# Causal attention on one Trainium2 core: scores, probabilities and their transposes cut to the visible keys

## What is computed

```python
def _causal_softmax(logits, q_pos, k_pos):
    mask = k_pos[None, :] <= q_pos[:, None]
    logits = jnp.where(mask, logits.astype(jnp.float32), -1e30)
    return jax.nn.softmax(logits, axis=-1)

# block 1, latent attention: 8 heads, 96 wide, values 64 wide, 272 keys
s = jnp.einsum('bqhd,bkhd->bhqk', qb, k) * scale
out = jnp.einsum('bhqk,bkhd->bqhd', _causal_softmax(s, q_pos, pos), v)
# block 1, differential attention: 4 heads of two 64-wide maps, values 128 wide, 272 keys
a = _causal_softmax(s1, q_pos, pos) - lam * _causal_softmax(s2, q_pos, pos)
# block 2, local attention: 8 heads, 64 wide, 256 keys, causal, with a distance bias
s_own = jnp.where(rel >= 0, s_own - sl * rel, -jnp.inf)
# block 2, cross attention: 4 heads, 64 wide, 256 memory keys, no mask
```

## Time and profile before

| what | us |
|---|---|
| median of three timed runs (lowest, highest) | 1489.84 (1487.89, 1492.24) |
| span of the profiled execution, first to last instruction | 1494.5 |
| first attention stage (mla, diff), about | 133 to 205 |
| moba heads, about | 1194 to 1227 |
| xattn heads, about | 1258 to 1280 |

### The profile page before, as it was taken

One profiled execution on the slowest core, in us unless ns is written; L12 is line 12 of the kernel. 1 busy time (PEld: TensorE's weight loads), 2 busy tenths in 40 slices (PEclk: granted clock), 3 DMA queues, 4 the chain that ended last, 5 costly groups with the idle time before them and its releaser, 6 DMA issues.

```text
span 1494.5 us, 31410 instructions
## 1 busy us (share of the span) xinstructions
PE 1434.7 (96%) x11038; PEld 1352.7 (91%) x11038; DVE 1016.9 (68%) x2084; ACT 684.3 (46%) x1035; POOL 557.1 (37%) x252
## 2 busy tenths in 40 slices
PE   6999998999899999999999999999999988999997
PEld 5787668999899999999999999999989957799997
DVE  4424544889888888877676666666555745599997
ACT  4432644445355555543333333444454345555553
POOL 3313227778800000024444444444423325254441
PEclk9989989999999999999999999999999978999999
DMA  7410125666655555557877777555553504256552
GB/s 278 142 58 29 43 85 176 191 192 192 185 194 175 175 175 175 176 185 228 238 230 232 232 230 229 177 190 182 183 171 120 175 20 144 76 186 188 184 174 80
DMA packets 89994, 250.16 MB, mean 167 GB/s; under 512 B 10048, under 2 KB 35920, under 8 KB 89296
## 3 DMA queue, kind: packets, MB, share of 16 engines
q1 hardware_dynamic: 86112, 238.20, 51.2%
q10 hardware_dynamic: 3824, 11.17, 2.1%
HBM read 234.09 MB, written 15.24 MB: 167 GB/s over the span
## 4 chain that ended last, share of the span: by engine, by line
PE 80%; DVE 6%; POOL 6%; issue 5%; ACT 1%; DMA 0%; ACTq 0%; POOLq 0%; DVEq 0%
PE ps L1651 37%; PE ps L2027 28%; POOL w_lo L494 6%; PE ps L2010 4%; PE ps L1915 2%; PE ps L1869 2%; PE ps L1666 1%; PE ps L1889 1%; PE ps L1840 1%; DVE big L1071 1%; DVE w_lo L1049 1%; PE ps L1730 1%; PE ps L1761 0%; ACT w_hi L595 0%; DVE big L1063 0%
## 5 line engine op out<-in xcount | busy, mean ns | idle before, releaser
L494 POOL TENSOR_TENSOR w_lo<-raw,w_hi 128x1024 fp32r<-128x1024 f32 x193 | 504.5, 2617 | 804.7 <-ACT w_hi L595 804.7
L1651 PE MATMUL ps<-x_op,w_hi 128*128 128x256 f32 (+1 forms) x3968 | 748.9, 290 | 22.0 <-DVE x_op L1067 8.8
L1651 PEld LDWEIGHTS ps<-x_op,w_hi 128*128 128x128 f32 x3968 | 627.2, 194 | 35.3 <-issue 20.5
L1651 PE MATMUL ps<-x_op,w_lo 128*128 128x256 f32 (+1 forms) x1984 | 567.2, 286 | 0.0
L595 ACT ACTIVATE w_hi<-raw 128x1024 fp32r<-128x1024 f32 x400 | 420.5, 1055 | 266.5 <-PE ps L2027 214.4
L2027 PE MATMUL ps<-h_op,w_hi 128*128 128x256 f32 x2400 | 426.7, 279 | 2.4 <-DVE h_op L1601 2.4
L1651 PEld LDWEIGHTS ps<-x_op,w_lo 128*128 128x128 f32 x1984 | 385.2, 194 | 0.0
L2027 PEld LDWEIGHTS ps<-h_op,w_hi 128*128 128x128 f32 x2400 | 367.8, 188 | 3.1 <-issue 1.8
L1049 DVE TENSOR_TENSOR w_lo<-raw,w_hi 128x1024 fp32r<-128x1024 f32 x207 | 265.4, 1282 | 114.2 <-ACT w_hi L595 114.0
L2027 PE MATMUL ps<-h_op,w_lo 128*128 128x256 f32 x1200 | 337.2, 281 | 0.0
L2027 PEld LDWEIGHTS ps<-h_op,w_lo 128*128 128x128 f32 x1200 | 225.2, 188 | 0.0
(11 more groups left out here) (267 smaller groups left out, 1057.6 us busy)
## 6 DMA issues: line engine op xcount, KB each, us to landing
raw<-blocks SPq DMA_DIRECT2D x404, 512.0 KB, 3.7
early_store<-kv_mem SPq DMA_DIRECT2D x96, 128.0 KB, 1.7
work<-early_store SPq DMA_DIRECT2D x96, 128.0 KB, 4.0
big<-consts ACTq DMA_DIRECT2D x2, 1336.0 KB, 6.6
big<-h_t ACTq DMA_DIRECT2D x4, 272.0 KB, 3.8
big<-bias_lines ACTq DMA_DIRECT2D x8, 136.0 KB, 2.6
bias_lines<-route_t ACTq DMA_DIRECT2D x4, 264.0 KB, 2.9
res<-mem_t SPq DMA_DIRECT2D x1, 1024.0 KB, 9.3
```

Source lines behind the costliest of these rows:

```text
L494: pool.tensor_tensor(w_lo[:, s, :], raw[:, s, :], w_hi[:, s, :].bitcast(F32), ALU.subtract).then_inc(sem("lo_pool"), 1)
L1651: mm = pe.matmul(ps[:, m_bank, 0:T], w, x, start=(k == 0 and j == 0), stop=(k == last and j == 2))
```

## The change

Two helper functions describe what a unit sees: `seen(u, t)` is the number of keys for query tile t (144 and 272 with 272 keys, 128 and 256 in moba, all 256 in xattn), and `key_tiles(u)` lists the tiles of keys, each with the first query that meets it, rounded down to a multiple of 32 (0, 96 and 224 with 272 keys; 0 and 128 in moba; 0 and 0 in xattn), and the column where its probabilities begin. Scores, mask or bias, maximum, exponential, normalisation and combination of query tile 0 work on `seen(u, 0)` keys. Instructions that took both query tiles at once become one for each tile. The transposed probabilities of all key tiles are packed side by side in bank 6 (448, 384 or 512 columns), and one copy moves them. `turn` with 272 keys has five transposes: two of 128 rows for key tile 0; for key tile 1 one of the last 32 rows of query tile 0 and one of 128 rows; and for the last 16 keys one of 32 rows. `weigh` runs over 256, 160 and 32 queries. Since 32 queries of tile 0 meet keys that they do not see, POOL clears columns 144 to 255 of the score buffers once.

```diff
+        def seen(u, t):
+            keys = units[u]["keys"]
+            return keys if units[u]["kind"] == "xattn" else min(keys, keys - NQ + P * (t + 1))
+        def key_tiles(u):
+            at = 0
+            for j in range(-(-units[u]["keys"] // P)):
+                if units[u]["kind"] == "xattn":
+                    first = 0
+                else:
+                    first = max(0, P * j - (units[u]["keys"] - NQ)) // 32 * 32
+                yield j, min(P, units[u]["keys"] - P * j), first, at
+                at += NQ - first
+        def probs_width(u):
+            return sum(NQ - first for _, _, first, _ in key_tiles(u))
...
-                    pool.tensor_tensor(s, s, row_inv[:, u % 3, :].unsqueeze(2).to_broadcast([P, 2, n]), ALU.mult
-                                       ).then_inc(sem("probs_normed"), 1)
+                    for t in range(2):
+                        s = scores_sb[:, u % 3, t, 0:seen(u, t)]
+                        ins = pool.tensor_tensor(s, s, row_inv[:, u % 3, t:t + 1].to_broadcast([P, seen(u, t)]), ALU.mult)
+                    ins.then_inc(sem("probs_normed"), 1)
...
+            pool.wait_ge(sem("q_sum"), 1)
+            pool.wait_ge(sem("k_sum"), 2)
+            pool.memset(scores_sb[:, :, 0, P + N_META:2 * P], 0.0)
             normalise(U_MLA, U_MOBA)
...
-                if x["keys"] > NQ:
-                    act.activation(probs_t[0:N_META, o % 2, 2, :], ps[0:N_META, out_bank(o), NQ:2 * NQ], ACT.Copy)
-                act.activation(flat2(probs_t[:, o % 2, 0:2, :]), ps[:, 6, :], ACT.Copy).then_inc(sem("probs_ready"), 1)
+                n = probs_width(u)
+                act.activation(probs_t[:, o % 2, 0:n], ps[:, 6, 0:n], ACT.Copy).then_inc(sem("probs_ready"), 1)
...
-                if o >= 2 and n > NQ:
-                    outputs_out(o)
-                for t in range(2):
-                    for j in range(2):
-                        mm = pe.transpose(ps[:, 6, j * NQ + t * P:j * NQ + t * P + P], scores_sb[:, u % 3, t, j * P:j * P + P], ident)
-                    if n > NQ:
-                        mm = pe.transpose(ps[0:N_META, out_bank(o), NQ + t * P:NQ + t * P + P], scores_sb[:, u % 3, t, NQ:n], ident)
+                for j, k, first, at in key_tiles(u):
+                    for t in range(first // P, 2):
+                        r = max(first - P * t, 0)
+                        a = at + P * t + r - first
+                        mm = pe.transpose(ps[0:k, 6, a:a + P - r], scores_sb[r:P, u % 3, t, P * j:P * j + k], ident[r:P, r:P])
                 mm.then_inc(sem("probs_turned"), 1)
...
-                    mm = pe.matmul(ps[rows, out_bank(o), 0:NQ], v, probs_t[0:k, o % 2, t, :], start=(t == 0), stop=(t == tiles - 1))
+                    mm = pe.matmul(ps[rows, out_bank(o), first:NQ], v, probs_t[0:k, o % 2, at:at + NQ - first],
+                                   start=(t == 0), stop=(P * t + k == x["keys"]), skip_group_check=True)
```

More of the change, by code:

```diff
@@ L782, in soft @@
                 for t in range(2):
+                    n = seen(u, t)
                     s = scores_sb[:, u % 3, t, 0:n]
@@ L1190, in soft_in @@
                 x = units[u]
-                n, b = x["keys"], 2 + 2 * (u % 2)
-                s = scores_sb[:, u % 3, :, 0:n]
-                src = ps[:, b:b + 2, 0:n]
+                b = 2 + 2 * (u % 2)
+                s = [scores_sb[:, u % 3, t, 0:seen(u, t)] for t in range(2)]
+                src = [ps[:, b + t, 0:seen(u, t)] for t in range(2)]
                 dve.wait_ge(sem("scores_done"), u + 1)
@@ L1205, in soft_in @@
                     for t in range(2):
-                        ins = dve.tensor_tensor_reduce(s[:, t], src[:, t], mask[:, t], 1.0, -3.0e38, ALU.add, ALU.max, m[:, t:t + 1])
+                        ins = dve.tensor_tensor_reduce(s[t], src[t], mask[:, t, 0:seen(u, t)], 1.0, -3.0e38, ALU.add, ALU.max, m[:, t:t + 1])
                     ins.then_inc(sem("scores_read"), 1)
@@ L1228, in soft_in @@
                     dve.wait_ge(sem("scores_read"), u + 1)
-                step(dve.tensor_reduce(m, s, AX.X, ALU.max))
+                    for t in range(2):
+                        ins = dve.tensor_reduce(m[:, t:t + 1], s[t], AX.X, ALU.max)
+                    step(ins)
                 dve.tensor_scalar(row_max[:, u % 3, :], m, -1.0, None, ALU.mult).then_inc(sem("max_ready"), 1)
@@ L1852, in scores @@
                 x = units[u]
-                h, n, b = x["head"], x["keys"], 2 + 2 * (u % 2)
+                h, b = x["head"], 2 + 2 * (u % 2)
                 if u >= 2:
@@ L1877, in turn @@
             def turn(u):
-                o, n = units[u]["out"], units[u]["keys"]
+                o = units[u]["out"]
                 if o is None:
@@ L1896, in weigh @@
                 x = units[u]
-                o, h, n = x["out"], x["head"], x["keys"]
+                o, h = x["out"], x["head"]
                 if o is None:
@@ L1903, in weigh @@
                 rows = slice(0, P) if x["kind"] == "diff" else slice(64 * (h % 2), 64 * (h % 2) + 64)
-                tiles = 3 if n > NQ else 2
-                for t in range(tiles):
-                    k = min(P, n - P * t)
+                for t, k, first, at in key_tiles(u):
                     if x["kind"] == "mla":
```

30 lines of the change are left out of this document (14 added, 16 removed).

## The result

The changed kernel takes 1505.33 us (median of 4 runs, 1502.81 to 1507.96) against 1489.78 of the kernel before: ratio 1.0103, 95% interval 1.0084 to 1.0122. It is slower by 15.5 us, and 25 over the forecast. The profiled run has a span of 1501.0 us, 6.5 more than before's. The two profiles differ by less than the medians because they lie at opposite ends: the one of the kernel before has a mean granted clock of 0.970, where its timed runs have mostly 0.977 to 0.980, and the one of the changed kernel is the fastest of its four runs.

What follows compares the result with a forecast made beforehand. PE, busy for 96% of the span, was taken to bound the kernel. Savings of 4.8 (mla heads, opening), 0.4 (diff), 1.4 (tail) and 3.0 (moba) made -9.6 us, from 1489.84 to about 1480, range 1473 to 1488.

Steps and rivals of the forecast that it cites:

- Rest: Everything outside the attention and moba savings: POOL's clearing, DMAs, SP's queue and xattn were to cost or gain nothing.
- The sum for moba: Moba heads fall from 4.95 to 3.88 us at half clock, the clock rising at the same moment (1214.2); -3.0 us.
- one more spell at half clock: Rival: fewer columns bring another half-clock spell, 7 to 8 us in mla and diff or 4 in moba; about 1488, chance 0.12.
- Its counter-argument: Against another half-clock spell: 64% busy from 138 to 142 kept clock 1.00, and the new mla head's columns fill 64%.
- The sign that the prediction named: A granted clock of 0.50 between 142 and 190, in the attention stage, would show the forecast wrong.
- The slower rival: The clock falls in the first mla heads and does not come back: +10.8 us, about 1500, chance 0.06.
- Parts 1 to 4: Mla head's transposes (0.71 to 0.94 us), scores, value product and copies: 2.89 in place of 3.39 us, boundaries included.
- POOL's split: POOL's multiply in two parts, priced at nothing, hidden under PE's mla head with 0.5 us to spare.
- Diff, tail: DVE's work in the diff heads, -0.4 us, and the half-clock tail of transposes, copies and value product, -1.4 us.

Runs made afterwards that it cites:

- e5: The changed kernel with one DVE maximum over both query tiles again in diff and moba heads, restoring DVE's instruction count ahead of the expand loop; 1491.85 us.
- e11: e5 plus filling matmuls: 3 ahead of each scores of the diff heads, 24 behind moba's second scores, 4 behind those of later moba heads; 1486.62 us.
- e14: The kernel before with the same filling matmuls as e11; 1494.51 us.
- e6: The changed kernel with DVE's expand loop written out over 8 blocks per turn in place of 4; 1495.20 us.
- e2: The changed kernel with 8 one-column memsets on DVE ahead of the expand loop; 1500.56 us.
- e3: The changed kernel with 24 one-column memsets on DVE ahead of the expand loop; 1505.83 us.
- e1: The kernel before with 8 one-column memsets on DVE ahead of the expand loop; 1505.07 us.
- e7: e5 plus four filling matmuls behind the scores of each next moba head, none more at moba's start; 1495.46 us.
- e13: e11 plus 12 more filling matmuls behind the second scores of the attention stage; 1486.63 us.

## Why the prediction was wrong

The 15.5 us split into three: +13.5 for the expansion (1505.33 less e5's 1491.85), +10 for the clock, -7.9 for the change's own work. The middle one is what is left (15.5 - 13.5 + 7.9 = 9.9, or 8 with the means of e11 and e14), and not measured by itself.

- **Rest: "Nothing".** This step failed, and it is the largest. It speaks of POOL's clearing, the DMAs, SP's queue and xattn, and not of the expansion, which cost 13.0 us: 8 DVE instructions more ahead of its loop made the loop's returns longer, and DVE's multiply fell behind POOL's subtraction. No row of before shows the code's position. What the trace did show is how thin the cover was: in the expansion of the kernel before, DVE's multiply starts 0.07 to 0.17 us ahead of POOL's subtraction in every second block. I never looked at a stage that the diff doesn't name.
- **The clock.** The sum for moba says "if the clock comes up at the same moment"; it didn't: half clock lasted to the end of the heads, 27 us. The rival "one more spell at half clock" priced just this at 7 to 8 in attention and 4 in moba, about 1488, at a chance of 0.12. It came in both stages; both prices on top of 1480.2 make 1491 to 1492, and e5, which has the clock's loss without the expansion's, took 1491.85. That the two agree so well is partly luck, since each price was rough. Its counter-argument set side by side a busy share (2.57 of 4.00 us) and a share of columns (1.85 of 2.89), both 64%, and these are not the same thing. The sign that the prediction named, 0.50 between 142 and 190, did show: until 145.28, and from 179.41. The slower rival named the first mla heads; they did run at half clock from 135 to 145, but the clock came back; that a time near its 1500 was measured has another cause.
- **Parts 1 to 4, the mla head.** Right to 0.02 us, boundaries included; POOL's split stayed under its cover: at full clock no head waited for POOL.
- **Diff, tail.** The head's DVE work couldn't be read apart from the clock. Together with mla the forecast was -6.6; e11 against e14 gives -5.0 by length and -2.7 by its end, with 12 us of half clock against 7 (0.94 and 0.97 of the stretch).
- **Moba.** -3.0 forecast, with the clock held -4.1; without fillers -0.2, in one profile each.

## What to carry to other kernels

A tight loop in which VectorE's two-input instruction and GpSimd's start within some tenths of a microsecond of each other is a loaded spring: eight instructions more ahead of it cost it 4.5% here. After an edit compare the stages that it does not touch first, and keep such a loop's returns few (e6 lost one block instead of eleven). And work cut from TensorE in a stage that already dips to half clock may be paid back in clock: look at the granted clock of the stage, and count a gain only if the clock is held; filling the idle stretch at moba's start held it there, but in the kernel before such fillers cost 4.5 us, so they have to be counted too.

## What the runs showed of the hardware

- The time that VectorE takes to return to the start of a loop depends on where its code lies. Subtraction to multiply over the first return took 0.54 us in the kernel before and 0.53 in e5, 0.70 in e2 and e3 (8 and 24 instructions further on than the changed kernel), 1.09 and 1.03 in the changed kernel and e1 (both 8 instructions behind before's place). Over the later returns it was 0.51, 0.65 and 0.74, and 0.34 without a return. What in the position decides was not tried.
- A first passage over straight code can stop VectorE as well: 0.61 us in e6 where no branch lies, 0.34 at the same place one turn later.
- A VectorE multiply of 0.42 us lasts 2.2 to 2.7 us when it starts behind a GpSimd subtraction of 2.4 us.
- With TensorE's columns cut, the clock was low for longer at the same busy share: PE was busy for 91% of the 27 us of moba at half clock (24.86 of 27.31), and for 90% of the 17 us in the kernel before (15.28 of 16.90). Four dense matmuls per head did not lift it in the profiled run of e7, and the same four with the idle start filled kept it from falling in e11 and e13.
